# One-core encoder trunk: first expert's tokens picked by matmul instead of gathered, half of the token scatter moved ahead, final sums ahead of the final norms

## The chip, the cores and the metric

The kernel runs on one core of one Trainium2 chip. The metric is device time in microseconds (us). The kernel before takes 631.53 us, the median of three runs (631.1 to 632.36). All times in this text are us unless marked ns. A core has the engines PE (TensorE, matrix products), DVE (VectorE), ACT (ScalarE), POOL (GpSimd) and SP (SyncE, which here only issues DMAs). Each runs its own instruction list in order and waits on semaphores for the others.

## The reference

512 tokens of width 1024 go through one layer and a final norm, all in f32:

```
h  = rms_norm(x);  proj = h @ w_in        # one input projection for three branches
x  = x + (sum over branches sigmoid(gate) * (branch @ w_br)) @ w_out
h2 = rms_norm(x, norm_ffn)
coarse = h2 @ w_coarse + b   (4 groups);  fine = h2 @ w_fine + b   (16 experts)
grp = argmax(coarse);  the 2 best experts of that group, by fine
w_top = softmax(those 2 fine values) * softmax(coarse)[grp]
y = sum over the 2 experts of w_top * (silu(h2 @ w_gate[e]) * (h2 @ w_up[e])) @ w_down[e]
out = rms_norm(x + y, final_norm)
```

w_gate and w_up are 16 x 1024 x 256, w_down is 16 x 256 x 1024. The branches (neighbourhood attention, a state-space layer, attention into 256 memory tokens) lie before the change and are untouched.

## The kernel before

**Precision.** A full-precision f32 product is made of three fast ones. ACT rounds each operand to a high part (`e_hi`, `xt_hi`, ...), DVE computes the rest (`e_lo`, `xt_lo`, ...) by a subtraction, and PE multiplies hi by hi, hi by lo and lo by hi (`split`, profile lines 1610 to 1612). So each weight passes ACT once and DVE once before PE can use it.

**Stages.** Up to about us 412 the branches are computed. Then `out_part` multiplies by w_out, four token tiles of 128 tokens each, the last until us 433. Beside it x2 (the new x) is added, squared and turned (`x2_turn`), the router's logits are computed, and `route` on DVE finds the two experts of each token. `places` on PE counts, by a product with a triangular matrix, at which place in its expert's list each token stands.

**Routing into lists.** Two ways exist to bring tokens to experts. For the first four experts (`NHOT`) a 0/1 table `hot` (slots by tokens) is made on DVE, PE multiplies it by token numbers (`slot_list`), and DVE turns the result into row numbers `idx0`. For the other twelve, POOL scatters (token, weight) pairs by indirect DMA into a DRAM table `tok_scratch` (8 DMAs, L2285), and reads it back as `idx` (L2293). The normed tokens stand in DRAM (`h_scratch`). POOL gathers the 128 rows of an expert into `xg` by an indirect DMA (L2269), and PE turns them (`tokens`, L1996).

**Expert loop.** `step(e)` on PE is: gate and up product of expert e, first half (12 products); turn the activations of e-1; turn the tokens of e+1; second half (12); down product of e-1 (12). ACT and DVE prepare hi and lo parts of one weight unit (1 MB) for each group of 12. Units come from SP in 9 buffers, in order of use: 0 and 1 are gate/up of expert 0, then three a step. POOL's loop copies the weights of the mixture (`wcur`), gathers expert e+3 and adds finished rows to `acc_scratch` (L423). The last two experts' rows are added by PE, with a table `hot_t` that POOL makes (L2304 to L2308).

**What sets the order.** Everything is written out by hand, engine by engine. Inside one engine nothing overtakes. SP starts unit 7 and those after it only when the gathers of experts 1 and 2 have landed.

**The end.** For each of four tiles DVE adds (`last_sum`), ACT squares and takes a root, DVE scales (`last_norm`), SP stores.

## Time and profile before

| what | value |
|---|---|
| median of 3 runs | 631.53 us |
| profiled execution, its own time | 630.6 us |
| its span, first to last instruction | 628.6 us |
| PE busy | 590.0 us, 94% |
| DVE busy | 420.2 us, 67% |
| ACT busy | 322.9 us, 51% |
| POOL busy | 214.3 us, 34% |
| moved by DMA | 111.62 MB |

The page was read from part 2 (slices of the span) to find where PE is not at its full share, then the timelines of each engine were read there. In the slices PE shows 8 tenths in four neighbouring ones, around us 425 to 490, and the granted clock 7 tenths in the slice that starts at us 471.5. The chain of waits then says which engine or DMA ended each wait. A row's time is when the instruction began on its engine. A matmul's shown duration includes its way through the array, so the time from one start to the next is what it costs.

### The profile page before, as it was taken

How to read it: one execution, taken by the hardware profiler on the slowest of the kernel's cores; microseconds unless marked ns; L12 is line 12 of the kernel's file. 1: busy time of each engine (PE TensorE's matmuls, PEld its weight loads, DVE VectorE, ACT ScalarE, POOL GpSimd, SP SyncE). 2: the span in 40 equal slices, each digit the busy share in tenths (PEclk: the TensorE clock that was granted, in tenths of full speed). 3: DMA queues.
4: the chain of work that ended last, by engine and by line, in shares of the span. 5: the costliest groups of instructions: out<-in, count | busy, mean ns of one | idle time of the engine just before them, and what ended most of it. 6: DMA issues, size and time to landing. Idle time of an engine off the chain costs nothing.

```text
span 628.6 us, 9094 instructions
## 1 busy us (share of the span) xinstructions
PE 590.0 (94%) x3190; PEld 474.9 (76%) x3190; DVE 420.2 (67%) x779; ACT 322.9 (51%) x537; POOL 214.3 (34%) x234
## 2 busy tenths in 40 slices
PE   3998999999999999999999999998888999999992
PEld 3887888889777777777777888885566888888771
DVE  4888214992477564555742388436896899999967
ACT  5864341221453434553252336224376899899853
POOL 3509987992001800000000000040653533556610
PEclk9999999999999999999999999999997999999996
DMA  9996424310432231222222227964699999999554
GB/s 295 165 244 174 116 68 136 99 36 7 142 122 69 65 100 68 68 68 67 68 68 79 91 100 184 353 238 151 215 331 411 361 381 384 387 387 382 141 109 173
DMA packets 89234, 111.62 MB, mean 178 GB/s; under 512 B 19614, under 2 KB 66880, under 8 KB 89193
## 3 DMA queue, kind: packets, MB, share of 16 engines
q1 hardware_dynamic: 79128, 93.65, 46.3%
q0 software_dynamic: 7280, 15.25, 9.2%
q10 hardware_dynamic: 2784, 2.18, 1.3%
q8 instruction: 24, 0.39, 0.3%
q14 instruction: 18, 0.14, 0.1%
HBM read 102.08 MB, written 14.75 MB: 186 GB/s over the span
## 4 chain that ended last, share of the span: by engine, by line
PE 74%; DVE 8%; DMA 6%; issue 4%; POOL 3%; ACT 3%; SPq 1%; DVEq 0%; POOLq 0%; ACTq 0%
PE bank L1610 20%; PE bank L1612 20%; PE bank L1611 19%; DMA xg<-h_scratch,idx 3%; PE bank L1792 2%; PE bank L1766 2%; PE bank L1779 2%; PE bank L1996 2%; DVE w_lo L1003 2%; DMA tok_scratch<-pay,rowi 1%; PE bank L1727 1%; PE bank L1905 1%; DMA x_sb<-in_x 1%; POOL tok_scratch L2285 1%; PE bank L1731 1%
## 5 line engine op out<-in xcount | busy, mean ns | idle before, releaser
L1003 DVE TENSOR_TENSOR w_lo<-raw,w_hi 128x1024 fp32r<-128x1024 f32 x55 | 74.2, 1349 | 105.2 <-ACT w_hi L575 104.7
L1610 PE MATMUL bank<-h_hi,w_hi 128*128 128x512 f32 x320 | 128.2, 401 | 1.5 <-DVE w_lo L1003 1.5
L1612 PE MATMUL bank<-h_hi,w_lo 128*128 128x512 f32 x320 | 124.9, 390 | 0.0
L1611 PE MATMUL bank<-h_lo,w_hi 128*128 128x512 f32 x320 | 124.6, 389 | 0.0
L1482 DVE TENSOR_TENSOR e_lo<-eraw,e_hi 128x2048 fp32r<-128x2048 f32 x47 | 106.5, 2292 | 8.1 <-ACT e_hi L813 8.1
L813 ACT CAST e_hi<-eraw 128x2048 fp32r<-128x2048 f32 x48 | 91.8, 1916 | 8.5 <-PE bank L1612 8.5
L575 ACT CAST w_hi<-raw 128x1024 fp32r<-128x1024 f32 x55 | 57.5, 1046 | 33.8 <-PE bank L1612 33.6
L1610 PEld LDWEIGHTS bank<-h_hi,w_hi 128*128 128x128 f32 x320 | 60.2, 188 | 13.7 <-DVE w_lo L1003 1.8
L1612 PEld LDWEIGHTS bank<-h_hi,w_lo 128*128 128x128 f32 x320 | 60.1, 188 | 13.1
L1611 PEld LDWEIGHTS bank<-h_lo,w_hi 128*128 128x128 f32 x320 | 60.2, 188 | 11.4
L2238 POOL TENSOR_TENSOR wcf<-wcf,prt 128x160 f32<-128x160 f32 x1 | 0.5, 459 | 195.5 <-DMA wcf<-in_moe_w_fine 195.5
L1610 PE MATMUL bank<-e_hi,xt_hi 128*128 128x512 f32 x128 | 52.4, 409 | 1.5 <-DVE e_lo L1482 1.0
L1612 PE MATMUL bank<-e_hi,xt_lo 128*128 128x512 f32 x128 | 50.8, 397 | 0.0
L1611 PE MATMUL bank<-e_lo,xt_hi 128*128 128x512 f32 x128 | 50.7, 396 | 0.0
L423 POOL DMA_INDIRECT acc_scratch<-ysb,idx x14 | 28.9, 2065 | 57.1 <-PE bank L1996 37.6
L673 ACT ACTIVATE gt<-bank,bgh 128x512 f32<-128x512 f32 x24 | 16.5, 689 | 43.4 <-PE bank L1612 43.4
L687 ACT ACTIVATE pr<-ssb,soft 128x192 f32<-128x192 f32 (+1 forms) x32 | 15.2, 475 | 30.3 <-DVE soft L1263 30.3
L1610 PEld LDWEIGHTS bank<-e_hi,xt_hi 128*128 128x128 f32 x128 | 24.7, 193 | 7.2 <-DVE xt_lo L1488 1.0
L1612 PEld LDWEIGHTS bank<-e_hi,xt_lo 128*128 128x128 f32 x128 | 24.5, 191 | 5.3
L1611 PEld LDWEIGHTS bank<-e_lo,xt_hi 128*128 128x128 f32 x128 | 24.6, 192 | 4.7
L2269 POOL DMA_INDIRECT xg<-h_scratch,idx x16 | 25.7, 1609 | 6.6 <-DVE idx L1477 3.4
L1610 PE MATMUL bank<-e_hi,at_hi 128*128 128x512 f32 x64 | 25.0, 391 | 1.1 <-DVE at_lo L1530 1.1
(401 smaller groups left out, 1235.0 us busy)
## 6 DMA issues: line engine op xcount, KB each, us to landing
raw<-in_w_in SPq DMA_DIRECT2D x40, 512.0 KB, 3.9
eraw<-in_moe_w_gate SPq DMA_DIRECT2D x32, 512.0 KB, 8.2
eraw<-in_moe_w_up SPq DMA_DIRECT2D x32, 512.0 KB, 12.7
eraw<-in_moe_w_down SPq DMA_DIRECT2D x32, 512.0 KB, 11.8
raw<-in_w_out SPq DMA_DIRECT2D x8, 512.0 KB, 3.8
x_sb<-in_x SPq DMA_DIRECT2D x4, 512.0 KB, 5.1
raw<-in_w_mem_kv SPq DMA_DIRECT2D x4, 512.0 KB, 15.6
raw<-in_w_br_na SPq DMA_DIRECT2D x4, 512.0 KB, 3.5
```

The costliest lines, as they stand in the source:

```text
L423: pool.indirect_dma_start(out=acc_dram, out_offset=bass.IndirectOffsetOnAxis(ap=v(idx, 2 * e, [1, 1]), axis=0), in_=v(ysb, D * (e % 2), [1 ...
L575: act.copy(v(dst, o, [1, 1024]), v(raw, 1024 * (c % RAW), [1, 1024])).then_inc(sem("w_hi_done"), 1)
L673: ins = act.activation(v(gt, SEQ * m, [1, SEQ]), pv(g % 2, 0, [1, SEQ]), ACT.Tanh, scale=0.5, bias=v(bgh, KD * branch + m, [1, 1]))
L687: ins = act.activation(v(pr, 512 * (p % 2) + 256 * j, [1, n]), src, ACT.Exp, bias=v(soft, so + 1, [1, 1]), accum_out=v(soft, so + 2, [1, 1]))
L813: act.copy(v(e_hi[dst], 0, [1, 2048]), v(eraw[j], 0, [1, 2048])).then_inc(sem("e_hi_done"), 1)
L1003: dve.tensor_tensor(v(l_, o, [1, 1024]), v(raw, 1024 * (c % RAW), [1, 1024]), raw32(v(h_, o, [1, 1024])), SUB).then_inc(sem("w_lo_done"), 1)
L1482: dve.tensor_tensor(v(e_lo[dst], 0, [1, 2048]), v(eraw[j], 0, [1, 2048]), raw32(v(e_hi[dst], 0, [1, 2048])), SUB).then_inc(sem("e_lo_done" ...
L1610: pe.matmul(dst, w[0], x[0], start=first, stop=False)
L1611: pe.matmul(dst, w[0], x[1], start=False, stop=False)
L1612: return pe.matmul(dst, w[1], x[0], start=False, stop=last)
L1766: ins = pe.matmul(pv(2 + j, 0, [1, n]), x, y, start=True, stop=True)
L2269: pool.indirect_dma_start(out=v(xg, D * (e % 3), [1, D]), out_offset=None, in_=h2_dram, in_offset=bass.IndirectOffsetOnAxis(ap=rows, axis= ...
```

## The change

- **First expert.** Its rows are no longer gathered. DVE makes its table as f32 (`hot0`), and PE multiplies h2 (f32) by it (`pick`): 8 column groups for each of 4 token tiles, 32 products. They replace the warm-up products between the router's steps and the eight transposes of expert 0.
- **Tables.** DVE makes only the tables of experts 0 and 1, POOL those of 2 and 3 (`table`, 8 instructions). `slot_list` runs for experts 1, 2 and 3; those of 2 and 3 lie inside step 0.
- **Scatter.** The weights of the mixture and the rows of tiles 0 and 1 are computed right after their routing (`weight_args`, `rows_of`, `weights`), and their 4 scatter DMAs are issued before h2's last tile is stored. The 4 of tiles 2 and 3 stay behind, two before and two after the gather of expert 3.
- **ACT** computes the exponentials in two parts, with two more loads of its function table. `first_lo(0)` on DVE moves ahead of the last half of x2.
- **SP** waits for `xt` (expert 0's tokens) and `xg1`, no longer for `xg2`.
- **POOL's table `hot_t`** is made in three pieces, in turns 4, 6 and 8 of its loop instead of all in turn 11.
- **The end.** All four sums come first, then roots and norms in pairs, and the last tile is stored in two halves.

The core of the diff:

```diff
+        def weights_exp(n0, nn):
+
+            act.wait_ge(sem("route_arg"), 2 if n0 else 1)
+            o = v(rt, 960 + 5 * n0, [1, 5 * nn])
+            act.activation(o, o, ACT.Exp).then_inc(sem("route_exp"), 1)
...
+        x2_take(NT - 1, 0)
+        weights_exp(0, 2)
+        act.activation(v(stat, 41, [1, 1]), v(stat, 48, [1, 1]), ACT.Sqrt)
         act.wait_ge(sem("last_out"), 3)
         unit_hi(0, 0, 1, 0)
-        x2_take(NT - 1, 0)
...
         xt_take(0, 0)
+        unit_hi(2, 2, 1, 2)
+        weights_exp(2, 2)
...
+        def weight_args(n0, nn):
+
+            for j in range(2):
+                dve.tensor_tensor(v(rt, 768 + 64 * j + 16 * n0, [16, nn], [NG4, PER], [1, NG4]),
+                                  v(rt, 640 + 64 * j + 16 * n0, [16, nn], [NG4, PER], [1, NG4]),
+                                  v(rt, 4 + 20 * n0, [20, nn], [1, PER], [PER, NG4]), MUL)
+            link(dve.tensor_reduce(v(rt, 908 + n0, [1, nn]), v(rt, 20 * n0, [20, nn], [1, 4]), AX.X, ALU.max))
+            link(dve.tensor_reduce(v(rt, 896 + n0, [4, 2], [1, nn]), v(rt, 768 + 16 * n0, [64, 2], [16, nn], [1, 16]),
+                                   AX.X, ADD))
+            dve.tensor_tensor(v(rt, 960 + 5 * n0, [5, nn], [1, 4]), v(rt, 20 * n0, [20, nn], [1, 4]),
+                              v(rt, 908 + n0, [1, nn], [0, 4]), SUB)
+            done(dve.tensor_tensor(v(rt, 964 + 5 * n0, [5, nn]), v(rt, 900 + n0, [1, nn]), v(rt, 896 + n0, [1, nn]),
+                                   SUB), "route_arg")
+
+        def weights(n0, nn):
+
+            dve.wait_ge(sem("route_exp"), 2 if n0 else 1)
+            dve.tensor_reduce(v(rt, 1012 + n0, [1, nn]), v(rt, 960 + 5 * n0, [5, nn], [1, 4]), AX.X, ADD)
+            link(dve.tensor_scalar(v(rt, 1016 + n0, [1, nn]), v(rt, 964 + 5 * n0, [5, nn]), 1.0, None, ADD))
+            link(dve.tensor_tensor(v(rt, 1012 + n0, [1, nn]), v(rt, 1012 + n0, [1, nn]), v(rt, 1016 + n0, [1, nn]), MUL))
+            link(dve.reciprocal(raw32(v(pay, 1 + 2 * n0, [2, nn])), v(rt, 1012 + n0, [1, nn])))
+            dve.tensor_tensor(raw32(v(pay, 9 + 2 * n0, [2, nn])), raw32(v(pay, 1 + 2 * n0, [2, nn])),
+                              v(rt, 964 + 5 * n0, [5, nn]), MUL).then_inc(sem("wts"), 1)
...
+        def first_hot(n0, nn):
+
+            dve.tensor_tensor(v(hot0, P * n0, [P, nn], [1, P]), v(slots, 0, [0, nn], [1, P]),
+                              v(rt, 1060 + NHOT * n0, [NHOT, nn], [0, P]), ALU.is_equal).then_inc(sem("hot"), 1)
...
-        place(0, NT - 1)
-        for e in range(NHOT):
-            one_hot(e, 0, NT - 1)
+        place(0, 2)
+        rows_of(0, 2)
+        weights(0, 2)
+        place(2, 1)
+        first_hot(0, NT - 1)
+        one_hot(1, 0, NT - 1)
+        dve.wait_ge(sem("e_hi_done"), 1)
+        first_lo(0)
         dve.wait_ge(sem("out_k"), NT)
...
             for j in range(2):
+                if isinstance(e, int) and e == 0 and j:
+                    first_lo(1).then_inc(sem("e_lo_done"), 1)
                 dve.wait_ge(sem("xt_hi"), 2 * e + j + 1)
                 dve.tensor_tensor(v(xt_lo[odd], 512 * j, [1, 512]), pv(4 + j, 0, [1, 512]),
                                   raw32(v(xt_hi[odd], 512 * j, [1, 512])), SUB).then_inc(sem("xt_lo"), 1)
...
+        slot_list(1)
+        xt_rest(0, 0)
+        unit_lo(1, 1, 1)
+        weight_args(2, 2)
+        rows_of(2, 2)
+        dve.wait_ge(sem("places"), 4)
...
+        slot_list(2)
+        weights(2, 2)
...
             if not peeled or e < 15:
+                xt_rest(e + 1, 1 - odd)
                 if peeled and e == 0:
                     unit_lo(2, 2, 2)
-                xt_rest(e + 1, 1 - odd)
...
+            if peeled and e == 0:
+                slot_list(3)
...
+        for n in range(NT):
             last_sum(n)
-            last_norm(n - 1)
-        last_norm(NT - 1)
+        for n in range(NT):
+            if n % 2 == 0:
+                inverse_root(NT + 4 + n // 2, n, 2)
+            last_norm(n)
...
             if c == C_OUT + 6:
+                places(2)
...
-                places(True)
-        warm(4, 3)
+        def pick(n, c):
+
+            return pe.matmul(pv(4 + c // 4, P * (c % 4), [1, P]), v(h2, D * n + c, [KD, P]), v(hot0, P * n, [1, P]),
+                             start=n == 0 and c % 4 == 0, stop=n == NT - 1 and c % 4 == 3)
+
+        pe.wait_ge(sem("hot"), 1)
+        parts = [(n, c) for c in range(KD) for n in range(NT - 1)]
+        for n, c in parts[:6]:
+            pick(n, c)
         x2_turn(NT - 1, 1)
-        warm(4, 3)
+        for n, c in parts[6:10]:
+            pick(n, c)
         logits(NT - 1, 1)
-        warm(4, 9)
-        places(False)
-        warm(4, 3)
-        for e in range(NHOT):
-            slot_list(e)
+        for n, c in parts[10:20]:
+            pick(n, c)
+        places(3)
+        for n, c in parts[20:]:
+            pick(n, c)
+        pe.wait_ge(sem("h2_scaled"), 1)
+        pe.wait_ge(sem("hot"), 2)
+        for c in range(4):
+            ins = pick(NT - 1, c)
+        ins.then_inc(sem("xt"), 1)
+        slot_list(1)
+        for c in range(4, KD):
+            ins = pick(NT - 1, c)
+        ins.then_inc(sem("xt"), 1)
         counts()
-        warm(0, 18)
...
+            first = isinstance(n, int) and n == 0
+            if not first:
+                pe.wait_ge(sem("e_lo_done"), n + 1)
             for k in range(4):
+                if first and k == 2:
+                    pe.wait_ge(sem("e_lo_done"), 1)
...
+            if first:
+                slot_list(2)
...
+                slot = (e0 + 1) % 3
+                tokens(e + 1, slot, 16 * (2 * i + (e0 + 1) // 3 + (1 if slot else 0)))
             if not peeled or e < 16:
                 gate_up(e, 1 if first else 3 * e, 1, 1 if first else 0, odd)
+            if first:
+                slot_list(3)
...
+        def table(e):
+
+            for n in range(NT):
+                ins = pool.tensor_scalar(v(hot, P * (NT * e + n), [1, P]), v(slots, P * e, [1, P]),
+                                         v(rt, 1060 + NHOT * n + e, [1, 1]), None, ALU.is_equal)
+            ins.then_inc(sem("iotas"), 1)
+
+        pool.wait_ge(sem("idx0"), 1)
+        gather(1)
+        pool.wait_ge(sem("hot"), 3)
+        table(2)
+        table(3)
+        pool.wait_ge(sem("idx0"), 2)
+        gather(2)
...
         store_x2(NT - 1)
...
+        pool.wait_ge(sem("rows"), 2)
+        pool.wait_ge(sem("wts"), 2)
+        scatter(2)
+        pool.wait_ge(sem("idx0"), NHOT - 1)
         pool.wait_ge(sem("xt"), 2)
         gather(3)
+        scatter(3)
```

PE, from the end of the last w_out product to the first product of expert 0. `onesb` rows are warm-up products, `x_sb` is x2, `selb` the chosen experts, `xg` gathered tokens. Before:

```order
L1913 MATMUL bank<-onesb 128x512 x3
L1895 MATMUL bank<-ident,x_sb 128x128 x4
L1913 MATMUL bank<-onesb 128x512 x3
L1905 MATMUL bank<-wcf,x2T 128x20 x4
L1913 MATMUL bank<-onesb 128x512 x9
L1927 MATMUL bank<-selb,upper 128x16
L1913 MATMUL bank<-onesb 128x512 x3
L1941 MATMUL bank<-tokf,hot 128x2 x16
L1933 MATMUL bank<-selb,onesb 128x16 x4
L1913 MATMUL bank<-onesb 128x512 x18
L1996 MATMUL bank<-ident,xg 128x128 x8
L1913 MATMUL bank<-onesb 128x512 x2
L1610 MATMUL bank<-e_hi_140,xt_hi_146 128x512
```

Now (`hot_164` is `hot0`, `h_177` is h2):

```order
L2028 MATMUL bank<-hot_164,h_177 128x128 x6
L1939 MATMUL bank<-ident,x_sb 128x128 x4
L2028 MATMUL bank<-hot_164,h_177 128x128 x4
L1949 MATMUL bank<-wcf,x2T 128x20 x4
L2028 MATMUL bank<-hot_164,h_177 128x128 x10
L1971 MATMUL bank<-selb,onesb 128x16 x3
L1972 MATMUL bank<-selb,upper 128x16
L2028 MATMUL bank<-hot_164,h_177 128x128 x8
L1990 MATMUL bank<-tokf,hot 128x2 x4
L2028 MATMUL bank<-hot_164,h_177 128x128 x4
L1978 MATMUL bank<-selb,onesb 128x16 x4
L1957 MATMUL bank<-onesb 128x512 x6
```

Picks stand where the warm-up products stood, the transposes of `xg` are gone, and of the 18 and 2 warm-up products at the end 6 are left.

DVE, between the lists' row numbers and the second expert's weights (`e_lo_143`, `144`, `145` are units 0, 1 and 2; `xt_lo_148` the tokens of expert 0, `149` of expert 1). Before:

```order
L1506 CAST rowi<-rt 128x8
...
L1428 TENSOR_TENSOR e_lo_143<-eraw_131,e_hi_140 128x2x512 x2
L1515 TENSOR_REDUCE rt<-rt 128x4
...
L1519 TENSOR_TENSOR pay<-pay,rt 128x4
L1488 TENSOR_TENSOR xt_lo_148<-bank,xt_hi_146 128x512 x2
L1482 TENSOR_TENSOR e_lo_144<-eraw_132,e_hi_141 128x2048
L1482 TENSOR_TENSOR e_lo_145<-eraw_133,e_hi_142 128x2048
L1488 TENSOR_TENSOR xt_lo_149<-bank,xt_hi_147 128x512 x2
```

Now:

```order
L1547 TENSOR_TENSOR xt_lo_148<-bank,xt_hi_146 128x512
L1481 TENSOR_TENSOR e_lo_143<-eraw_131,e_hi_140 128x2x512
L1547 TENSOR_TENSOR xt_lo_148<-bank,xt_hi_146 128x512
L1539 TENSOR_TENSOR e_lo_144<-eraw_132,e_hi_141 128x2048
L1437 TENSOR_TENSOR rt<-rt 128x32 x2
...
L1466 CAST rowi<-rt 128x2x2
...
L1534 SCALAR_TENSOR_TENSOR idx_170<-bank,rt 128x1
...
L1455 TENSOR_TENSOR pay<-pay,rt 128x2
L1547 TENSOR_TENSOR xt_lo_149<-bank,xt_hi_147 128x512 x2
L1539 TENSOR_TENSOR e_lo_145<-eraw_133,e_hi_142 128x2048
```

The weights' and rows' small instructions for tiles 2 and 3 and a slot list now stand between units 1 and 2, and unit 2 stands behind the tokens of expert 1.

POOL, from the last store of h2 to the gather of expert 4, before:

```order
L2243 DMA h_scratch<-h_176 128x1024
L2269 DMA xg<-h_scratch,idx_169 128x1024 x3
L2247 DMA acc_scratch<-x_sb 128x1024
L2285 DMA tok_scratch<-pay,rowi 8192x2 x8
L2269 DMA xg<-h_scratch,idx_169 128x1024
L2293 DMA idx<-tok_scratch 32x32 x4
L2297 COPY wcur<-idx 128x1 x2
L2269 DMA xg<-h_scratch,idx 128x1024
```

Now:

```order
L2342 DMA tok_scratch<-pay,rowi 8192x2 x4
L2318 DMA h_scratch<-h_177 128x1024
L2357 DMA xg<-h_scratch,idx_170 128x1024
L2366 TENSOR_SCALAR hot<-slots,rt 128x128 x8
L2357 DMA xg<-h_scratch,idx_170 128x1024
L2322 DMA acc_scratch<-x_sb 128x1024
L2342 DMA tok_scratch<-pay,rowi 8192x2 x2
L2357 DMA xg<-h_scratch,idx_170 128x1024
L2342 DMA tok_scratch<-pay,rowi 8192x2 x2
L2387 DMA idx<-tok_scratch 32x32 x4
L2391 COPY wcur<-idx 128x1 x2
L2357 DMA xg<-h_scratch,idx 128x1024
```

Four scatters moved ahead of the store, one gather is gone, the eight table instructions came in, and the gather of expert 3 stands between the last two pairs of scatters.

## Rows read from the trace of the kernel before

**Rows 1.** The chain of waits, us 440 to 500: start us, us, what
```profile
442.19 4.53 DMA xg<-h_scratch,idx
...
461.23 8.02 DMA tok_scratch<-pay,rowi
...
469.54 2.20 POOL idx L2293 x4
...
477.10 9.03 DMA xg<-h_scratch,idx
```

**Rows 2.** Timeline, PE: start us, us, instruction, idle before and releaser
```profile
448.88 0.50 PE L1610 MATMUL bank<-e_hi,xt_hi 128*128 128x512 f32 x1 [0.52 <-DVE xt_lo L1488]
...
455.37 0.39 PE L1610 MATMUL bank<-e_hi,xt_hi 128*128 128x512 f32 x1
...
472.47 1.97 PE L1996 MATMUL bank<-ident,xg 128*128 128x128 f32 x8 [3.10 <-DMA xg<-h_scratch,idx]
474.10 0.78 PE L1610 MATMUL bank<-e_hi,xt_hi 128*128 128x512 f32 x1
...
478.08 0.47 PE L1610 MATMUL bank<-e_hi,xt_hi 128*128 128x512 f32 x1
...
486.25 1.15 PE L1996 MATMUL bank<-ident,xg 128*128 128x128 f32 x8 [1.54 <-DMA xg<-h_scratch,idx]
487.16 0.48 PE L1610 MATMUL bank<-e_hi,xt_hi 128*128 128x512 f32 x1
...
492.72 0.39 PE L1610 MATMUL bank<-e_hi,xt_hi 128*128 128x512 f32 x1
```

**Rows 3.** Windows: stretch, us, busy us of engines, granted clock, DMA share, GB/s
```profile
472.00:478.00 6.00, 5.53 (x17) 4.75 (x18) 2.49 (x3) 3.96 (x5) 1.20 (x3) 0.50 1.03 417
```

**Rows 4.** Timeline, DVE, us 430 to 456
```profile
433.98 0.68 DVE L1381 TENSOR_TENSOR x_sb<-bank,x_sb 128x512 f32<-128x512 f32 x1
...
440.06 0.90 DVE L1422 TENSOR_TENSOR hot<-slots,rt 128x128 bf16<-128x128 f32 x4
...
441.91 0.44 DVE L1494 TENSOR_TENSOR rt<-rt 128x64 f32<-128x64 f32 x2
...
444.38 2.36 DVE L1428 TENSOR_TENSOR e_lo<-eraw,e_hi 128x1024 fp32r<-128x1024 f32 x2
...
449.34 4.48 DVE L1482 TENSOR_TENSOR e_lo<-eraw,e_hi 128x2048 fp32r<-128x2048 f32 x2
453.74 1.28 DVE L1488 TENSOR_TENSOR xt_lo<-bank,xt_hi 128x512 fp32r<-128x512 f32 x2
```

**Rows 5.** Timeline, ACT, us 427 to 441
```profile
427.94 1.91 ACT L813 CAST e_hi<-eraw 128x2048 fp32r<-128x2048 f32 x1 [0.88 <-PE bank L1612]
...
439.74 1.28 ACT L864 ACT_TABLE_LOAD   x1
```

**Rows 6.** Timeline, PE, us 141 to 142, f32 products of 128 by 128
```profile
141.00 0.39 PE L1727 MATMUL bank<-st_im,ca 128*128 128x128 f32 x2
141.23 0.39 PE L1727 MATMUL bank<-st_re,ca 128*128 128x128 f32 x2
```

**Rows 7.** Timeline, POOL, us 448 to 456
```profile
449.70 2.78 POOL L2285 DMA_INDIRECT tok_scratch<-pay,rowi  x1 [0.30 <-issue]
...
454.97 0.97 POOL L2285 DMA_INDIRECT tok_scratch<-pay,rowi  x1 [0.30 <-issue]
```

**Rows 8.** Timeline, POOL, us 572 to 577
```profile
573.44 2.65 POOL L2305 CAST rt<-idx 128x2 f32<-128x2 int32 x1
```

**Rows 9.** Timeline, PE, us 589 to 590
```profile
589.58 1.04 PE L1996 MATMUL bank<-ident,xg 128*128 128x128 f32 x7 [0.60 <-DMA xg<-h_scratch,idx]
```

**Rows 10.** Timeline, DVE, us 612 to 629
```profile
612.65 2.48 DVE L1589 TENSOR_TENSOR xf<-bank,xf 128x512 f32<-128x512 f32 x4 [1.55 <-PE bank L2089]
...
624.24 1.28 DVE L1596 SCALAR_TENSOR_TENSOR xf<-xf,stat,gfin 128x1024 f32<-128x1024 f32 x1
```

**Rows 11.** DMA issues, us 616 to 629: tile, queue, count, KB, us to landing
```profile
out<-xf SPq DMA_DIRECT2D x4, 512.0 KB, 2.6
```

More of the change, by code:

```diff
@@ L861, in _ @@
         unit_hi(1, 1, 1, 1)
-        act.wait_ge(sem("route_arg"), 1)
-        act.activation(v(rt, 960, [1, 20]), v(rt, 960, [1, 20]), ACT.Exp).then_inc(sem("route_exp"), 1)
+        act.activation(v(stat, 41, [1, 1]), v(stat, 48, [1, 1]), ACT.Exp)
         def xt_take(e, odd):
@@ L2045, in step @@
                 ins.then_inc(sem("e_used"), 1)
-        tokens(0, 0, 16)
-        warm(0, 2)
         for e in range(3):
```

166 lines of the change are left out of this document (79 added, 87 removed).

## Prediction

> **What bounds the kernel now.** I read the slices of the page first: PE is short of its full share only around us 430 to 490 and after 610. Then, for that stretch, the chain of waits, the timelines of PE, DVE, ACT and POOL, and one window for the clock. The chain is to be read as three DMA round trips. Expert 0's rows are gathered from 442.19 and land 4.53 later. The last scatter is issued at 461.23 and lands 8.02 later, then the table is read back (469.54), and only then can expert 4's rows be gathered at 477.10, landing after 9.03 [rows 1]. PE shows the same from its side [rows 2]: its first expert product starts at 448.88, expert 1 at 455.37, it waits 3.10 for expert 3's rows until 472.47 and 1.54 for expert 4's until 486.25, and expert 4's own products start at 492.72. From there the loop runs without such gaps but for one of 0.60 at 589.58 [rows 9]. The clock row says that after the 3.10 gap the granted clock was 0.50, the lower level of 1.2 GHz [rows 3].
>
> So two points decide what happens before 492.72: when PE may start, and when expert 4's rows have landed. What is won ahead of the second is lost again if the second doesn't move.
>
> **The start of expert 0.** Removed: slot list, gather and transposes of expert 0. Added on the path: the last eight picks. A product of f32, 128 by 128, costs 0.23 from one start to the next [rows 6]; the same form is what a pick is, so 24 picks are 5.4, laid where the 18 warm-up products ahead of the lists were and partly in PE's wait for the last half of x2; eight are 1.8. h2's columns are read with a step of 8, so 0.2 to 0.45 each is the bound; I take 0.23.
>
> ACT pays first. Its Exp for tiles 0 and 1 needs two table loads of 1.28 [rows 5], and they now stand ahead of the cast of unit 0 (1.91), which before began at 427.94. With x2's copy, the two loads and the two short activations ahead of it, about 4 in all, it begins near 432.0 and ends near 433.9. DVE now waits for this cast before `first_lo(0)`, half of the 2.36 of [rows 4], so 1.2, and behind that stands the last half of x2. It began at 433.98 and will begin at 435.0: 1.0 late, although DVE makes two tables there and not four. Everything after it, x2's turn, the logits, `route`, `place`, comes 1.0 later. The tables of the last tile began at 440.06 [rows 4], now 441.1. PE's four picks then run 441.5 to 442.4, the list of expert 1 and four more picks to 443.6, and counts and six warm-up products (0.23 each) until 445.1. ACT and DVE have the first half of the tokens split by 443.9, so the warm-up products hide behind nothing and set the start: 445.1 instead of 448.88, 3.8 early.
>
> **Until expert 1.** DVE takes it back. From the first half of `xt_lo` at 443.2 it has: tokens 1.3 [rows 4], `first_lo(1)` 1.2, unit 1 2.25 (half of 4.48), then the small routing instructions of tiles 2 and 3 (2.4, the stretch from 441.91 to 444.38 in [rows 4]; fewer columns hardly shorten instructions this small), a slot list and the weights (1.2, seven at 0.17), then tokens of expert 1 1.3, unit 2 2.25. The sum is 11.9, so unit 2 is ready at 455.1. Expert 1 started at 455.37: of 3.8 won, 0.3 is left. PE idles some 2 to 3 before it. Expert 0's own wait for POOL's table of expert 2 costs under 1 and is covered by the same gap.
>
> **Until expert 4.** POOL's queue decides. Its gather of expert 2 waits for the list, which DVE writes at 450.6, behind the small instructions, against 441 before; the eight table instructions end about then too. Then come, in order: gather 2, the store, two scatters, gather 3 (its list is written about 456.2), one scatter, and the last scatter. An indirect DMA costs POOL 0.97 and 0.30 to the next when nothing is in its way, and 2.78 at 449.70, where DVE was subtracting a weight unit: it ended 0.9 after the first of the two units of 449.34 did [rows 4, 7]. A copy of two columns took 2.65 in the same way [rows 8]. So an issue that meets a unit waits for the unit's end. By the free price the last scatter starts at 459.6; if each of the last four meets a unit, at 463.2. Four of eight scatters were moved ahead, but a gather, a table and a later start came in: I take 461.0, against 461.23.
>
> The Trainium skill (SBUF — State Buffer, section "SBUF: two separate sides") speaks against the change here: the port pair of VectorE and GpSimd is an exclusive lock, held for a whole instruction, and descriptors from GpSimd's queue can't be written while VectorE holds it. The two long rows agree with it, 2.78 against 0.97. By it the new instructions on POOL are the dear ones; without it the last scatter would be at 459.6.
>
> From the last scatter's start to the next gather's start 15.9 went by (461.23 to 477.10) [rows 1], which gives 476.9 again. The gather's landing took 9.03 under full DMA load (share 1.03 [rows 3]), and 4.53 at 442.19 without. PE will stand still then, so DVE and the weight loads are a little behind it; I take 8.1, near the loaded row. Expert 4's rows are there at 485.0, 1.25 early. Bounds: 480 (free issues and a light queue) to 488.5 (463.2, and the rest as before).
>
> PE comes to this point early: expert 1 at 455.1, gather 2 landed near 459, expert 2 at 465.4, expert 3 at 475, its first half done at 478. It then waits 7 in place of 1.54. After 3.10 of idle time the clock was at its lower level until 478.08, so this longer wait will end cold too. Cold, the eight transposes took 1.63 (472.47 to 474.10), against 0.91 (486.25 to 487.16), and nine products 3.98 (474.10 to 478.08), against 9 x 0.228 = 2.05: 2.65 more [rows 2]. Before, this price was paid in expert 3's gap and hidden by the next wait; now it stands behind the last wait, and nothing hides it. Expert 4's products: 485.0 + 6.47 (486.25 to 492.72) + 2.65 = 494.1, that is 1.4 later than before.
>
> **After it.** POOL's `hot_t` in three pieces no longer pushes one gather: the 0.60 goes [rows 9]. Cost of the pieces in turns 4, 6 and 8: nothing, since POOL waits some us in each turn for finished rows; if that cover is gone, up to 3.
>
> **The end.** DVE's four sums run on without a gap, 2.48 for two [rows 10]: 612.65 to 617.6. Then a paired root (five small instructions, 0.9), norms 0 and 1 (1.25 each), a root, norm 2, and the halves of norm 3: 617.6 + 0.9 + 2.5 + 0.9 + 1.25 + 1.3 = 624.4, against 624.24 + 1.28 = 625.5. ACT's squares run beside it. The last store is half as large; 512 KB took 2.6 [rows 11], moving at about 400 GB/s, so 0.65 less. Together 1.7; bounds 0.5 (the first stores start 2.3 later and could pile up) to 2.0.
>
> **Sum.** +1.4 - 0.6 - 1.7 = -0.9. The profiled execution took 630.6 (span 628.6 and 2.0 around it), so 629.7; the median of the runs shown is 0.9 above it, so 630.6.
>
> **Rivals.**
> - *The chain really is shorter.* Most issues fall between DVE's units and the backlog of weights is gone when the gather runs. For: the four early scatters, and units 7 and later start about 2.5 sooner. Against: POOL's later start. Rows at 482.5: -1.1 - 2.3 = -3.4, 628.1.
> - *The last scatters come late.* The two after gather 3 meet units 4 and 5 on DVE, and their packets stand behind its 512 KB. The port rule above is this case. Rows at 488: +4.4 - 2.3 = +2.1, 633.6. It decides against the kernel from 486.9 on, where the losses pass the 2.3 of the end. For: in the schedule above the second scatter begins within 0.1 of unit 3.
> - *The wait is so short that the clock holds*, rows at 480 to 481: -6 - 2.3, about 623.5. Against: all DMAs would have to be free.
> - *The change doesn't do what it says:* picks of 0.4, or more waits, keep expert 0 at 448. Then PE's slack before expert 4 takes it: -0.9 again.
>
> **How the numbers follow.** Forecast with the last rival 0.48 (its own range 629.0 to 632.0), shorter chain 0.27, late scatters 0.20, no cold clock 0.05. This kernel can tell 0.2%, 1.3 us, from no change. Faster by more: 0.27 + 0.05 and 0.12 of the forecast, 0.44. Slower: 0.20 of the late scatters and 0.02 of the forecast, 0.22. Same: 0.34. The range that leaves out 2 in 10 is 627.0 to 633.5.
>
> **What would show it.** First expert product near 445; expert 1 near 455; one long wait of PE at expert 4's transposes and a granted clock of 0.5 after it; the last scatter near 461; last DVE row 1.1 earlier against PE's last product. It is wrong if the last scatter is before 458 or after 464, if PE's long wait is at another expert, or if PE doesn't get cold.

## The result: 0.86% slower, outside the forecast

The changed kernel takes 636.6 us (median of 12 runs, 634.09 to 641.53), the kernel before 631.47 in the same comparison (12 runs, 630.12 to 634.47). The ratio is 1.0086, 95% interval 1.0069 to 1.0104: 5.1 us slower. The prediction said 630.6, range 627.0 to 633.5. The profiled execution took 635.16, its span is 633.5. One execution of `e14_turned_order` below, 638.97 at a mean granted clock of 0.978 where its others had 0.985 to 0.992, is left out of its median.

The page of the changed kernel, its span, busy times, and slices of PE and the clock:

```profile
span 633.5 us, 9156 instructions
PE 595.3 (94%) x3212; PEld 485.0 (77%) x3212; DVE 420.8 (66%) x785; ACT 326.0 (51%) x540; POOL 214.2 (34%) x241
...
PE   3998999999999999999999999999969999999992
...
PEclk9999999999999999999999999999989999999997
```

Where the kernel before had four slices at 8 tenths, there is one at 6, from us 459.3 to 475.1, and the clock's dip (8) in the same slice.

PE's timeline of the changed kernel (start, us, engine, line, op, count, idle before and its releaser) answers to [rows 2, 9]:

```profile
433.08 0.40 PE L1656 MATMUL bank<-wp_hi,m_lo 128*128 128x512 f32 x1
433.48 3.12 PE L2028 MATMUL bank<-hot,h 128*128 128x128 f32 x12
...
440.04 5.00 PE L2028 MATMUL bank<-hot,h 128*128 128x128 f32 x20
444.88 0.22 PE L1971 MATMUL bank<-selb,onesb 128*128 128x16 bf16 x3
...
444.99 4.05 PE L2028 MATMUL bank<-hot,h 128*128 128x128 f32 x16
448.88 0.24 PE L1990 MATMUL bank<-tokf,hot 128*128 128x2 bf16 x4
...
452.17 0.58 PE L1654 MATMUL bank<-e_hi,xt_hi 128*128 128x512 f32 x1
...
456.76 0.25 PE L1990 MATMUL bank<-tokf,hot 128*128 128x2 bf16 x4 [1.49 <-POOL hot L2366]
...
469.64 1.88 PE L2064 MATMUL bank<-ident,xg 128*128 128x128 f32 x8 [4.52 <-DMA xg<-h_scratch,idx]
...
492.64 1.16 PE L2064 MATMUL bank<-ident,xg 128*128 128x128 f32 x8 [1.34 <-DMA xg<-h_scratch,idx]
...
595.57 1.05 PE L2064 MATMUL bank<-ident,xg 128*128 128x128 f32 x8
```

The records at L2028 are the picks, two for one product. Sixteen of them fill 444.99 to 448.88: 0.243 each, 0.486 for a pick. The first expert product starts at 452.17 and not near 445; the long wait is expert 2's (4.52) and not expert 4's (1.34). The wait of 0.60 near 589 is gone (595.57 shows none). After the 4.52, the granted clock is at its lower level, as in [rows 3]; a window of that stretch (columns as in [rows 3]):

```profile
470.00:473.00 3.00, 3.00 (x12) 2.64 (x11) 1.38 (x2) 2.03 (x3) 0.00 (x0) 0.50 1.04 409
```

The chain of waits of the changed kernel, answering to [rows 1]:

```profile
431.64 1.28 ACT L865
...
440.20 4.85 PE bank L2028 x20
445.13 3.91 PE bank L2028 x16
...
450.43 2.01 POOL xg L2357
452.49 5.13 POOL hot L2366 x6
457.84 0.76 POOL hot L2366 x2
...
459.18 10.41 DMA xg<-h_scratch,idx
469.64 1.88 PE bank L2064 x8
```

It is to be read downwards: ACT's second table load, then the picks, then POOL's gather of expert 1, its eight table instructions, and only then the gather of expert 2, which takes 10.41 to land. Weights from SP are under way by then: over us 459.2 to 469.6 the DMA share is 0.99, at 355 GB/s. The change let SP start units without waiting for expert 2's rows (`xg2`), so it is itself a possible cause of this slow landing. No run puts that wait back, and what it costs or gains isn't shown. POOL's timeline (L2366 the tables, L2342 the scatters), answering to [rows 7]:

```profile
450.43 2.01 POOL L2357 DMA_INDIRECT xg<-h_scratch,idx  x1 [9.50 <-DVE idx L1534]
452.49 6.53 POOL L2366 TENSOR_SCALAR hot<-slots,rt 128x128 bf16<-128x128 f32 x8
459.18 1.08 POOL L2357 DMA_INDIRECT xg<-h_scratch,idx  x1 [0.17 <-issue]
460.26 0.61 POOL L2322 DMA_DIRECT2D acc_scratch<-x_sb  x1
...
464.27 1.97 POOL L2357 DMA_INDIRECT xg<-h_scratch,idx  x1 [0.30 <-issue]
466.55 1.84 POOL L2342 DMA_INDIRECT tok_scratch<-pay,rowi  x1 [0.30 <-issue]
468.69 0.97 POOL L2342 DMA_INDIRECT tok_scratch<-pay,rowi  x1 [0.30 <-issue]
```

The end, DVE's timeline, answering to [rows 10]:

```profile
618.53 2.48 DVE L1630 TENSOR_TENSOR xf<-bank,xf 128x512 f32<-128x512 f32 x4 [1.55 <-PE bank L2164]
621.29 2.49 DVE L1630 TENSOR_TENSOR xf<-bank,xf 128x512 f32<-128x512 f32 x4 [0.28 <-DMA xf<-acc_scratch]
...
627.80 2.61 DVE L1639 SCALAR_TENSOR_TENSOR xf<-xf,stat,gfin 128x1024 f32<-128x1024 f32 x3
```

**A common zero.** What lies ahead of the picks ended at different times in the profiles. PE's last product with w_out (433.08 above, called the last product of the branches in what follows) began at 432.68 in the kernel before and between 431.45 and 434.42 in the others, and one kernel profiled twice had 433.79 and 431.84. Traces are therefore compared from that product on (a plus sign marks a time from it):

| kernel | its start | first expert product | last scatter | expert 4's transposes | end of span | timed ratio, 95% |
|---|---|---|---|---|---|---|
| before | 432.68 | +16.20 | +28.55 | +53.57 | +195.92 | 1 |
| changed | 433.08 | +19.09 | +35.61 | +59.56 | +200.42 | 1.0086, 1.0069 to 1.0104 |
| `e4_late` | 434.27 | +19.10 | +41.47 | +65.01 | +207.53 | 1.016, 1.0133 to 1.0186 |
| `e10b_after_order` | 434.41 | +19.09 | +33.37 | +58.57 | +201.49 | 1.006, 1.004 to 1.008 |
| `e5_dvetab` | 431.45 | +19.10 | +35.04 | +58.95 | +202.45 | 1.0061, 1.0034 to 1.0087 |
| `e1_step1` | 431.49 | +12.89 | +31.91 | +55.20 | +198.81 | 1.0009, 0.9988 to 1.003 |
| `e2_turned` | 432.15 | +13.07 | +32.02 | +54.39 | +197.45 | 0.9999, 0.9976 to 1.0022 |
| `e6_noload` | 433.96 | +11.55 | +30.34 | +52.40 | +195.24 | 0.9964, 0.9945 to 0.9984 |
| `e8_turned_dvetab` | 431.89 | +13.09 | +30.62 | +54.18 | +196.51 | 0.9989, 0.9971 to 1.0006 |
| `e14_turned_order` | 434.37 | +13.07 | +28.23 | +52.10 | +195.43 | 0.9969, 0.9949 to 0.9988 |
| `e9_order` | 431.55 | +13.08 | +27.12 | +50.75 | +194.85 | 0.9905, 0.9883 to 0.9928 |
| `e9c_order` (same kernel) | 431.65 | +13.07 | +29.36 | +54.39 | +194.85 | 0.9929, 0.9904 to 0.9955 |
| `e11b_warm` | 433.79 | +13.08 | +27.98 | +51.83 | +193.31 | 0.9975, 0.9962 to 0.9989 |
| `e11c_warm` (same kernel) | 431.84 | +13.08 | +27.97 | +53.45 | +195.86 | 0.9967, 0.9943 to 0.9992 |
| `e3_end` | 432.56 | +16.23 | +28.58 | +52.94 | +195.84 | 0.9988, 0.997 to 1.0005 |
| `e7b_endhot` | 431.84 | +16.27 | +28.62 | +52.79 | +195.46 | 0.9983, 0.9964 to 1.0002 |

Of the 4.9 between the two spans, 0.4 lies before the zero and 4.5 behind it. Each row of the table is one execution. The two rows of the kernel `e11b_warm` end 2.5 apart (193.31 and 195.86), so a difference in the column "end of span" that is smaller than that says little; for the total the timed ratios count.

### The profile page after: what moved, and what is told of

Same layout as the page of the kernel before. It is cut to its first block, busy times and chain, and to the rows that moved or that the text cites. A ratio compares the mean times of both kernels' runs of the same rounds, so it can differ in the third digit from the quotient of the medians.

```text
span 633.5 us, 9156 instructions
## 1 busy us (share of the span) xinstructions
PE 595.3 (94%) x3212; PEld 485.0 (77%) x3212; DVE 420.8 (66%) x785; ACT 326.0 (51%) x540; POOL 214.2 (34%) x241
## 4 chain that ended last, share of the span: by engine, by line
PE 69%; DVE 9%; DMA 7%; SPq 6%; ACT 3%; issue 3%; POOL 1%; DVEq 0%; ACTq 0%; POOLq 0%
PE bank L1654 18%; PE bank L1656 18%; PE bank L1655 18%; DMA xg<-h_scratch,idx 3%; PE bank L1836 2%; DVE w_lo L1016 2%; DMA raw<-in_w_mem_kv 2%; PE bank L1823 2%; PE bank L1810 2%; PE bank L2064 2%; PE bank L2028 2%; PE bank L1771 1%; SPq L495 1%; DMA xf<-acc_scratch 1%; SPq L474 1%
```

## The experiments

**The price of a pick.** `e1_step1` reads other columns of h2 and changes nothing else:

```diff
-            return pe.matmul(..., v(h2, D * n + c, [KD, P]), v(hot0, P * n, [1, P]),
+            return pe.matmul(..., v(h2, D * n + P * c, [1, P]), v(hot0, P * n, [1, P]),
```

> The changed kernel with one edit: the picks read h2's columns side by side (step 1) and not with a step of 8. Expert 0 then multiplies its tokens' columns in the wrong order; the work is the same in number and size. Main theory (the step makes each pick dear, and the picks set the start of expert 0): a pick costs 0.23 us instead of 0.485, so the count of tile 3 is no longer late; it begins near 442.4 instead of 444.9, the first expert product begins 4 to 5 us earlier (near 447.4 instead of 452.2), the gather of expert 1 about 4 earlier, and the whole kernel takes 3.0 to 5.0 less than the changed one: 631.6 to 633.6. Rival A (the chip charges f32 products of this shape 0.48 whatever the step): pick 0.48, time unchanged, 636.6. Rival B (POOL's queue decides and the picks are beside the path): picks 0.23, first product earlier, but the last scatter stays near 468.7 and the time is within 1 of 636.6.

Measured: 632.41 us, 1.0009 of before. The weight loads of the changed kernel and of this one, by source line (duration min/median/max, first and last start, forms):

```profile
L2028 PEld LDWEIGHTS bank<-hot,h x64: 312/335/336, 433.5 to 450.6; 128*128 128x128 f32 x64
```

```profile
L2028 PEld LDWEIGHTS bank<-hot,h x64: 186/192/193, 431.9 to 442.9; 128*128 128x128 f32 x64
```

PE's timeline of `e1_step1`:

```profile
437.60 2.48 PE L2028 MATMUL bank<-hot,h 128*128 128x128 f32 x20
439.92 0.23 PE L1971 MATMUL bank<-selb,onesb 128*128 128x16 bf16 x3
...
444.38 0.58 PE L1654 MATMUL bank<-e_hi,xt_hi 128*128 128x512 f32 x1
```

The ten picks from 437.60 to 439.92 take 2.32; those from 440.04 to 444.88 in the changed kernel took 4.84. The main theory's 4 to 5 us at the first product were too little (6.2, from +19.09 to +12.89), its 3.0 to 5.0 in time held (4.2 by the medians, 0.0077 or 4.9 by the ratios; the single traces end 1.6 apart). Rival A falls with the price of a pick, rival B with the time and the last scatter, which came 3.7 earlier.

`e2_turned` is the same gain with the right result: h2 is written in the order in which PE reads it, and the gathered rows then stand in that order too.

```diff
-            dve.scalar_tensor_tensor(v(h2, D * n, [1, D]), v(x_sb, D * n, [1, D]), ..., v(gffb, 0, [1, D]), MUL, MUL)
+            dve.scalar_tensor_tensor(v(h2, D * n, [1, P], [P, KD]), v(x_sb, D * n, [KD, P], [1, KD]), ..., v(gffb, 0, [KD, P], [1, KD]), MUL, MUL)
...
-                    ins = pe.transpose(pv(4 + j, P * k, [1, P]), v(xg, D * slot + 4 * j + k, [KD, P]), ...)
+                    ins = pe.transpose(pv(4 + j, P * k, [1, P]), v(xg, D * slot + P * (4 * j + k), [1, P]), ...)
```

> The changed kernel with h2 written in SBUF in the order in which PE reads it (DVE writes with a step of 128 elements, so that column d = 8p + k stands at 128k + p). Picks and the transposes of all experts then read side by side; nothing is left out. Main theory: the same gain as with the picks alone read side by side, 3 to 5 us, plus at most 0.3 from the transposes, which showed no cost of the step (0.11 us each): 631.3 to 633.6. Rival: DVE's writes with a long step are slower, each of the three products of 1024 elements by 1.1 us or more (twice the time), and the last tile's products sit on the path: then x2's turn and all behind it come about 0.5 to 1 later, and the gain is 1 smaller than that of the run with the picks alone.

Measured: 631.31 us, 0.9999. Both were partly right: DVE's product with the gain, 512 elements, took 1.07 to 1.10 instead of 0.69 (of 1024 elements 2.00 to 2.10 instead of 1.28), and the first product is 0.18 later than without it; the time doesn't show it. So mending the picks takes away what the change had lost, as far as the runs can tell (5.3 us between the two medians), and gains nothing over the kernel before.

`e12b_steps` measures the price by step, two of the eight column groups at each of 1, 2, 4 and 8 (`[(1, 2, 4, 8)[c // 2], P]` for `[KD, P]`).

> The changed kernel with the eight column groups of the picks read with steps of 1, 1, 2, 2, 4, 4, 8, 8 elements; expert 0 then gets some wrong columns. It measures the price of a pick by step, not the kernel's time. Theory A (any step but 1 is dear): 0.225 at step 1, 0.485 at 2, 4 and 8. Theory B (the price grows with the bytes that the reads span): 0.225, about 0.23 to 0.3 at 2, 0.3 to 0.4 at 4, and 0.485 at 8.

One execution, 637.4 us. Its weight loads in windows that hold steps of 1, 2, 4 and 8 in this order (line, op, count, busy us, mean ns, idle before):

```profile
L2028 PEld LDWEIGHTS bank<-hot,h 128*128 128x128 f32 x12 | 1.4, 191 | 0.4 <-DVE hot L1470 0.4
```

```profile
L2028 PEld LDWEIGHTS bank<-hot,h 128*128 128x128 f32 x8 | 1.0, 199 | 0.0
```

```profile
L2028 PEld LDWEIGHTS bank<-hot,h 128*128 128x128 f32 x8 | 1.9, 327 | 0.0
```

```profile
L2028 PEld LDWEIGHTS bank<-hot,h 128*128 128x128 f32 x4 | 1.1, 335 | 0.0
```

Neither theory: 191 and 199 ns at steps of 1 and 2, 327 and 335 at 4 and 8. The picks follow the loads: the four at a step of 2 take 0.96 from start to start (438.67 to 439.63), 0.24 each, and a stretch of two such picks, six at 4 and two at 8 takes 4.31 (440.53 to 444.84), which leaves 0.48 for one at 4. A step of two f32 is nearly free here, and 4 costs about what 8 does.

**POOL's tables.** `e5_dvetab` is the changed kernel with `for e in range(1, NHOT): one_hot(e, ...)` on DVE and without `table(2)`, `table(3)` on POOL.

> The changed kernel with the 0/1 tables of experts 2 and 3 made by DVE again (two more instructions for tiles 0 to 2, two more for tile 3) and not by POOL. Main theory (POOL's eight table instructions, 6.5 us on the profile, hold up the lists of experts 2 and 3 and gather 2): PE's wait of 1.5 for POOL's table is gone, gather 2 is issued at 457 to 458 instead of 459.2, the last scatter moves from 468.7 to about 467, and the kernel takes 1 to 2.5 less: 634.1 to 635.6. Rival (DVE writes the list of expert 2 late anyway, behind its small routing instructions, and pays for four more): gather 2 stays at 459.2 or later, time within 0.7 of 636.6 or above it.

Measured: 635.53 us, 1.0061, within the main theory's range, but its interval overlaps that of the changed kernel, and from the common zero on its one trace is 2.0 longer. PE's wait for POOL's table is gone, and gather 2 is issued 1.3 earlier (+24.80 for +26.10), after 5.42 of waiting for DVE's list; the last scatter is 0.6 earlier only, and PE waits 5.85 for expert 4's rows. With picks this late no gain from the tables can be told from none.

`e8_turned_dvetab` does the same to the turned version.

> The turned version with the tables of experts 2 and 3 made by DVE; nothing is left out. Main theory (both costs were real and both are now gone): PE's wait of 2.4 for POOL's table is gone and with it the low clock behind it, gather 2 is issued about 1.5 earlier (451.6 for 453.2), the last scatter near 462.6, and the time is 1 to 2 less than the turned version's, 0.998 of the kernel before. Rival (DVE's four more instructions sit on its path): no more than 0.3 gained.

Measured: 631.43 us, 0.9989: no gain that can be told from the turned version's 0.9999. Its trace says why:

```profile
450.76 1.09 PE L2067 MATMUL bank<-ident,xg 128*128 128x128 f32 x8 [2.58 <-DMA xg<-h_scratch,idx]
455.77 0.47 PE L1658 MATMUL bank<-e_hi,xt_hi 128*128 128x512 f32 x1 [1.07 <-DVE e_lo L1543]
...
486.07 1.96 PE L2067 MATMUL bank<-ident,xg 128*128 128x128 f32 x8 [5.91 <-DMA xg<-h_scratch,idx]
```

The 2.40 for POOL's table became 2.58 for expert 1's rows, which land only then; and all that PE won until expert 3 ends in 5.91 for expert 4's rows. The last scatter, 1.4 earlier, was near the 462.6 of the main theory (462.51), but the gain of 1 to 2 didn't follow.

**The scatters.** `e4_late` moves the four early scatters back behind gather 2.

> The changed kernel with the four early scatters put back behind gather 2 and the store, in a row with the other four (two of them stay behind gather 3). Main theory (POOL's chain to the last scatter sets when expert 4's rows come, and four DMAs ahead of it cost at least 4 x 1.27 us): the last scatter moves from 468.7 to 474 or later, expert 4's rows come 5 later, PE waits that much longer there, and the time is 3 to 5.5 more than the changed kernel's: 639.5 to 642. Rival (the table is read back late for another reason, or PE has slack behind): time within 1 of 636.6.

Measured: 642.87 us, 1.016. The last scatter is 5.9 later, expert 4's rows 5.5, PE waits 5.94 for them, and the kernel is 6.3 slower than the changed one by the medians (7.1 by the traces), a little above the range. So this idea of the change holds: inside it, the early scatters are worth about 6 us.

`e10b_after_order` leaves all as changed but for two lines, the last scatters ahead of the gather of expert 3:

```diff
         scatter(2)
+        scatter(3)
         pool.wait_ge(sem("idx0"), NHOT - 1)
         pool.wait_ge(sem("xt"), 2)
         gather(3)
-        scatter(3)
```

> The changed kernel, picks with step 8 and POOL's tables as they are, with only the last two scatters put ahead of the gather of expert 3. Main theory (expert 4's rows come one chain after the last scatter): the last scatter moves from 468.7 to about 466.5, and PE's wait of 1.34 for expert 4's rows goes, so the time is 1 to 1.5 less than the changed kernel's; more isn't there, since PE's own late start then decides. Rival (expert 3's rows become late): a new wait at expert 3's transposes, no gain.

Measured: 635.25 us, 1.006. The last scatter is 2.2 earlier and the wait of 1.34 is gone, as expected; the median is 1.35 below the changed kernel's, but the intervals overlap. The trace shows no gain either: PE now waits 1.31 for expert 5's rows, and from the common zero on it is 1.1 longer.

`e9_order` puts turned h2, DVE's tables and this order together.

> As the turned version with DVE's tables, and the last two scatters put ahead of the gather of expert 3; nothing is left out. Main theory (the last scatter is the start of the chain to expert 4's rows): it begins 1.5 to 2.5 earlier, expert 4's rows come as much earlier, expert 3's rows come 2 later but before PE wants them, and the time is 1 to 2 less than without this edit. Rival (gather 3 comes late and PE waits for expert 3's rows instead): no gain, or up to 1 slower.

Measured: 626.18 us (5 runs, 625.83 to 628.19), 0.9905. It was run again beside two others:

> The fastest version (h2 turned, DVE's tables, last scatters ahead of gather 3) again, on one chip with the two below. From PE's last product of the branches to the end its profile showed 194.85, against 195.92 of the kernel before and 200.42 of the changed one; by that it is 0.998 of before, by its five timed runs 0.9905. Theory A (the 0.9905 was partly how the branches' part, which varies by 2 us between kernels and runs, fell in those five): 0.993 to 0.998 now. Theory B: 0.9905 again.

Measured: 627.2 us (6 runs, 626.07 to 628.61), 0.9929 (0.9904 to 0.9955), between the two theories. This is the fastest kernel here, and beats both. POOL and PE in its first profile:

```profile
457.40 0.96 POOL L2345 DMA_INDIRECT tok_scratch<-pay,rowi  x1 [0.30 <-issue]
458.67 0.96 POOL L2345 DMA_INDIRECT tok_scratch<-pay,rowi  x1 [0.30 <-issue]
459.94 2.92 POOL L2360 DMA_INDIRECT xg<-h_scratch,idx  x1 [0.30 <-issue]
```

```profile
450.73 1.97 PE L2067 MATMUL bank<-ident,xg 128*128 128x128 f32 x8 [2.89 <-DMA xg<-h_scratch,idx]
...
482.30 1.09 PE L2067 MATMUL bank<-ident,xg 128*128 128x128 f32 x8 [0.61 <-DMA xg<-h_scratch,idx]
...
493.72 1.51 PE L2067 MATMUL bank<-ident,xg 128*128 128x128 f32 x8 [1.91 <-DMA xg<-h_scratch,idx]
```

The last scatter at 458.67 met no unit of DVE (it began in none of DVE's subtractions of a weight unit), and expert 4's rows were there at 482.30, +50.75; the prediction's rival of a shorter chain had 482.5, which is +49.8. In the second profile two scatters met units (3.08 and 3.07), the last came 2.2 later and expert 4's rows 3.6 later; yet both profiles end at +194.85, and expert 7's transposes start at +82.40 and +82.31. So what is won at expert 4 is partly given back before expert 7: the first profile waits 1.91 for expert 5's rows, with the lower clock behind it. From the common zero on this kernel is only 1.1 shorter than before, while the timed runs say 4 to 6. Part of the gap is which execution was profiled: 630.6 against a median of 631.5 for the kernel before, but 628.19 against 626.18 and 628.34 against 627.2 here. Another 1.0 to 1.1 lies before the zero. Where in the kernel the rest was won stays open.

`e14_turned_order` keeps POOL's tables.

> h2 turned and the last scatters ahead of gather 3, but POOL's tables of experts 2 and 3 as in the changed kernel. What the tables cost by themselves once picks and order are mended. Theory A (the eight instructions hold gather 2 and the scatters): last scatter 1.5 later than with DVE's tables, 0.5 to 2 us slower than that version. Theory B (the order of the scatters was all): within 0.5 of it.

Measured: 629.18 us, 0.9969 (0.9949 to 0.9988): 2.0 slower than `e9c_order` by the medians, last scatter 1.1 later than in the first profile of that kernel, 1.1 earlier than in the second. Theory A by the medians, but the intervals overlap. Against the turned version's 0.9999 (0.9976 to 1.0022) the order alone gained about 0.3%, again with intervals that overlap. With DVE's tables the same two lines gained 0.8% (`e8_turned_dvetab` to `e9_order`, in one comparison), 0.6% by `e9c_order`, and there the intervals are apart.

**Clock.** `e11b_warm` adds `warm(2, 11)` ahead of expert 1's transposes to the fastest version.

> The fastest version so far (turned, DVE's tables, scatters first) with 11 dummy products of 512 columns put in PE's wait of 2.9 for expert 1's rows, so that the clock doesn't fall behind it. Theory A (after the picks are cheap, expert 4's rows decide, and what PE wins before is lost there): expert 1's second start and expert 2 are 1 to 2 earlier, PE's wait of 0.6 for expert 4's rows grows by as much, and the time is within 0.5 of that version's. Theory B (PE's own chain decides there): 1 to 2 less.

> That version with 11 dummy products in PE's wait for expert 1's rows. Its profile showed 193.31 over the same stretch, 1.5 less than without them (the first expert after the wait at full clock), though its timed runs stood higher in another call. Theory A: 0.5 to 1.5 less than the version without, in the same call. Theory B (expert 4's rows take it back): within 0.5.

Measured: 629.96 us (0.9975), and beside `e9c_order` 628.97 us (0.9967, 0.9943 to 0.9992), 1.8 above that kernel's median. The dummies did their work in the trace: the granted clock over us 450 to 456 is 1.00, where without them 452 to 458 had 0.61.

```profile
450.00:456.00 6.00, 6.00 (x37) 4.06 (x34) 5.14 (x23) 1.29 (x3) 2.47 (x3) 1.00 0.63 184
```

```profile
452.00:458.00 6.00, 6.00 (x23) 4.70 (x22) 3.75 (x4) 1.71 (x4) 5.09 (x4) 0.61 0.96 313
```

But PE then waited 2.25 for expert 2's rows, and no time came back; the gain of theory B in the first text, A in the second, didn't come. The two traces are no help: from the common zero on one ends 1.5 earlier than `e9c_order`, the other 1.0 later. So no gain from the full clock ahead of a later wait can be told. Why the version was, if anything, slower isn't settled.

**ACT's table loads.** `e6_noload` is the turned version with `ACT.Exp if n0 else ACT.Identity` and without the square root's reload behind it.

> The turned version (h2 in the order in which PE reads it) with ACT's first exponentials replaced by a plain copy, so that both table loads of 1.28 between x2's copy and the cast of unit 0 go; the weights of tiles 0 and 1 are then not the softmax's. Main theory (the loads put the last half of x2 back by 1.0, and with picks of 0.23 that is on the path): PE's wait of 1.75 for that half falls to about 0.8, the last half of x2 begins 1.0 earlier (434.2 for 435.2 of the turned version), the first expert product 1.0 earlier, and the time is 0.5 to 1 less than the turned version's. Rival (behind it POOL's queue and the table read-back take it): first product earlier, time within 0.3 of the turned version's.

Measured: 629.75 us, 0.9964. The first product is 1.5 earlier than in the turned version (+11.55 for +13.07), expert 4's rows 2.0 earlier, the time 1.6 less by the medians (631.31, from another comparison). That is more than expected, but the intervals of the two ratios overlap (0.9945 to 0.9984, 0.9976 to 1.0022), so that it reached the end is likely and not shown. The last half of x2 began at +1.49, near the +1.30 of the kernel before: the loads are what puts it back.

**The end and the last experts' table.** `e3_end` and `e7b_endhot` give these to the kernel before.

> The kernel before with only the new end: four sums first, roots and norms in pairs, last store in two halves. By the prediction's own step: 1.7 less than before, bounds 0.5 to 2.0, so 629.8. By what the changed kernel's trace shows (from the first sum to the end 14.97 against 15.95): 1.0 less, 630.5. Rival (the stores pile up behind one another and give it back): within 0.3 of 631.5.

> The kernel before with the new end and with POOL's table for the last two experts made in three pieces, nothing else. By the terms as now measured (end 1.0, and 0.6 from PE's wait at 589 that the long piece caused) it takes 1.6 less than before, ratio 0.9975; by the prediction's terms (1.7 and 0.6) 2.3 less. Rival (the pieces cost POOL time in turns 4 to 8 and push a gather there): a new wait of PE for expert rows between 495 and 560, and no gain beyond that of the end.

Measured: 631.96 us, 0.9988, and 629.72 us, 0.9983. Neither can be told from no change. In the traces the end, from DVE's first sum to the span's end, is 15.30 and 15.65 against 15.95 before [rows 10] and 14.97 in the changed kernel. Where the sums run on without a norm between them, DVE waits for the rows of `xf`, 0.86 in `e7b_endhot` and 0.57 in `e3_end`:

```profile
616.15 2.50 DVE L1594 TENSOR_TENSOR xf<-bank,xf 128x512 f32<-128x512 f32 x4 [0.57 <-DMA xf<-acc_scratch]
```

In `e3_end` PE waited 1.92 near us 590, where the long piece of `hot_t` stood, and in `e7b_endhot` not at all; no new wait came in turns 4 to 8.

## Why the prediction was wrong

**The step that failed: "the same form is what a pick is ... I take 0.23".** A pick costs 0.486. [Rows 6] have the same shape, but their weights stand side by side. The prediction saw the step of 8 and set bounds of 0.2 to 0.45 from nothing but that row; the measured price lies above them. Yet the kernel before held a nearer row, half a microsecond behind the one read. The weight loads of its lines 1731 (step 16) and 1727 (step 1), and one group of such loads in the timeline:

```profile
L1731 PEld LDWEIGHTS bank<-upk,mg x32: 294/310/313, 141.6 to 154.5; 128*128 128x128 f32 x32
```

```profile
L1727 PEld LDWEIGHTS bank<-st_re,ca x32: 187/192/205, 140.6 to 153.6; 128*128 128x128 f32 x32
```

```profile
141.57 0.95 PEld L1731 LDWEIGHTS bank<-upk,mg 128*128 128x128 f32 x4
...
142.42 0.32 PEld L1727 LDWEIGHTS bank<-st_re,ca 128*128 128x128 f32 x2
```

From the first load of two such products to the next product's, 0.85 passes, 0.43 a product: nearly twice the 0.23 that was taken, and near the upper bound (the moving operand has 64 columns here, a pick's has 128).

**And the place of the picks.** The prediction counted eight on the path. At 0.486, the ten between the logits and the count for tile 3 are on it too: the count began at 444.88, +11.80, in `e1_step1` at 439.92, +8.43. Together the first product came at +19.09; +12.4 was predicted (445.1), and the mended kernels had +12.89 and +13.07. The rival with picks of 0.4 said that expert 0 stays at 448 and PE's slack takes it. Expert 0 came 2.9 later than before instead, and no slack took it: POOL's queue, gather 1 first, hangs on the list that PE makes behind the picks. Gather 1 was issued at +17.35, in `e1_step1` at +12.16. What failed, then, is the price of the picks and the step from it to "PE's slack takes it": 4.2 to 4.9 of the 6.0 between forecast and result are gone once the picks read side by side.

**What the mended kernel says of the rest.** With the picks alone mended, the ratio is 1.0009 and 0.9999, and the forecast, -0.9 us, is 0.9986: inside the interval of `e2_turned`, just below that of `e1_step1` (from 0.9988). That its total comes so near is partly luck, since its parts fared as follows.

- ACT's loads put the last half of x2 back by 1.0: right in kind, too small. It began at 436.10, +3.02, for +1.30 before [rows 4], 1.7 later; DVE's `first_lo(0)` waited 1.06 for the cast. Without the loads it is 1.5 earlier (`e6_noload`); whether the end gains by it isn't shown.
- Expert 1 near 455.1, so +22.4: in `e1_step1` 455.43, at +23.94. PE's wait for POOL's table, "under 1 and covered", was 2.40, with the lower clock behind it.
- POOL's tables: 6.5 for eight, seven at 0.59 and one of 2.43 that lay in DVE's unit of 452.39. The prediction had "about then" for their end, near 450.6 (+17.9), and gather 2 behind it. The gather came at 459.18 (+26.1), and with the picks mended at +20.8 and +21.0. The eight instructions were never priced from a row.
- The last scatter near 461.0 (+28.3): +35.6, mended +31.9. Two causes, the late start and gather 3 ahead of two scatters (3.08 where it met a unit, in both kernels with mended picks). The upper bound of 463.2 (+30.5) was added up too low as well: at the row's own 2.78 for 0.97, three issues that meet a unit ahead of the last scatter give 459.6 + 5.4 = 465.0.
- What makes an issue long was told by a rule that the rows bear out in part. The Trainium skill (SBUF — State Buffer, section "SBUF: two separate sides"), which the prediction cites for it, says that GpSimd can't write descriptors while VectorE runs in one of its two-port modes; DVE's units are subtractions of two inputs, and no run here shows in which mode they ran. The rows show this much: an indirect DMA begun within a unit took up to 3.08 and one outside 0.96 to 1.08, a table instruction 2.43 and 0.59, but the plain store at 460.26, within the unit of 459.48 to 461.76, took 0.61, as elsewhere (0.58). Not everything on POOL waits.
- One long wait at expert 4's transposes with the low clock behind it: not in the changed kernel, where it was expert 2's; but in `e1_step1` 3.37 and a granted clock of 0.61 over us 484 to 490, and in `e8_turned_dvetab` 5.91. The mechanism was right for the kernel that the prediction had in mind, its size wasn't: a wait of 7 was forecast, and `e1_step1` has another of 3.26 at expert 2. Expert 4's rows came at +55.2 and +54.4 with the picks mended, where the forecast had +52.3 and the rival of late scatters +55.3; yet the time wasn't the 2.1 longer of that rival. (Its limit of 486.9 should be 485.9: 485.0 plus the 0.9 by which 2.3 exceeds 1.4.)
- `hot_t`: the wait is gone, 0.6 as said; its cost in other turns nothing, as said.
- The end: 1.0 in the trace for 1.7. DVE's part nearly held: from the first sum to the end of the last norm it took 11.88 (618.53 to 630.41) for 12.87 before, 0.99 less for 1.1, although it waits 0.28 for `xf`. The term that failed is the 0.65 for the half store. From DVE's end to the span's end 3.09 passed, and 3.08 before; the last store, half as large, still took 2.7 to land, where [rows 11] had 2.6:

```profile
out<-xf SPq DMA_DIRECT2D x2, 256.0 KB, 2.7
```

## What to carry to other kernels

A product's price is that of its form with its access pattern: look in the trace for a row with the same step on the same operand, and if a bound is given without one, let the range hold twice the price. Count work that is put into idle time at its highest price before calling it hidden, since filler ahead of a latency-bound step becomes the path as soon as it is longer than the gap. In a queue that works in order, put the instruction that starts the longest chain first: here moving two scatters ahead of a gather took 0.6 to 0.8% off the kernel whose tables DVE made, while moving the tables alone took off 0.1%, which can't be told from nothing.
